# Modulation rows of a two-layer trunk: two short ones in the first stage, the other twenty groups streamed through the first projection

## The chip, the core and the metric

The kernel runs on one core of a Trainium2 chip, in fp32 throughout. The metric is device time in microseconds (us), the median of several executions. The profiler records one execution; a time in its views counts from the start of that execution's span. The engines are TensorE (PE), VectorE (DVE), ScalarE (ACT), GpSimd (POOL) and SyncE (SP), which issues most DMAs here, in program order, and waits in place on semaphores.

## The reference

One step through two layers. For each layer and both condition vectors (one for the 128 prompt tokens, one for the 512 latents) a long vector is made once: six rows of 1024 values.

```
def adaln(cvec, w, b):
    m = jax.nn.silu(cvec) @ w + b
    return jnp.split(m[:, None, :], ADA_CHUNKS, axis=-1)     # w: 1024 x 6144 per layer
...
for l in range(DEPTH):
    mp = adaln(c_ctx[None, :], ada_w[l], ada_b[l])
    ms = adaln(c, ada_w[l], ada_b[l])
    hp = modulate(xp, mp[0], mp[1])                          # x * (1 + scale) + shift
    hs = modulate(xs, ms[0], ms[1])
    ...                                                      # layer 0: mLSTM mixer, layer 1: GLA mixer
    xp = layer_norm(DEEPNORM_ALPHA * xp + mp[2] * yp, ln_mix_g[l], ln_mix_b[l])
    fp = peer_ffn(modulate(xp, mp[3], mp[4]), ...)
    xp = layer_norm(DEEPNORM_ALPHA * xp + mp[5] * fp, ...)
```

Rows 0 and 1 (shift and scale) are wanted at the start of a layer, rows 2 to 5 only after its mixer. `ada_w` is 25.2 MB for each layer.

## The kernel before

The program is a sequence of stages, each with its own semaphores, separated by a barrier of all engines: `mod0` (`modulation_rows`), `proj0`, the mLSTM scan, `out0` (`mixer_output`), `peer0`, then `proj1`, the GLA scan, `out1`, `peer1`. 640 tokens make `NT` = 5 tiles of 128.

`modulation_rows` makes all six rows of layer 0. For each of 12 groups of 512 columns SP loads 128x8x512 of `ada_w` (2 MB) into one of the two slots `m.W[:, s]`, and waits for `ps_full` before it loads a slot again. TensorE multiplies by `cs`, the silu of the two condition vectors (two columns used of 32), in 4 blocks of 128 columns that go to the four 32-column groups of the array: 8 x 4 matmuls of 128x32 by 128x128 a group (L188). VectorE adds the bias (L217). At the end the constants, the tokens `X` (L166 to L168) and the stored rows (L172) close the stage.

`project` (L221) loads the shift and scale rows, broadcast to 128 partitions (L243), modulates each tile on VectorE (L264, L267), transposes it on TensorE (L277, copied by ScalarE, L322), and multiplies it by the weights `w_in`, 6 groups of 512 columns of 2 MB each in the same two slots `m.W` (L249). A unit, below, is one tile by one group: 8 matmuls with 512 columns (L293), 30 units in all, group by group. A slot's next load is issued as soon as `ps_full` says that the group in it is done, one group ahead of its use. Last come the gates (L304). Before unit 0, 1, 2 and 3 TensorE also transposes the next tile. VectorE has nothing to do once the five tiles are modulated.

`mixer_output` normalises each tile on VectorE (`head_norm`), transposes it, multiplies by `w_out` (L825) and adds it to the residual (`residual`: L912 to L915, then the layer norm). In layer 0 it also makes all six rows of layer 1 (`more`): 24 groups of 256 columns of `ada_w`, three slots of 1 MB (L787), 6 groups a tile on TensorE (L839), bias on VectorE (L923); before the stage ends the rows are stored (L797). In layer 1 it does not.

Every fp32 matmul stands in the trace as two records, so a unit is 16 records of L293, and a group of 32 matmuls is 64 records of L188.

Of the kernel before, what the change touches and what calls it, by code (L numbers as in the profile page):

```python
# [18 lines left out]
ALU = mybir.AluOpType  # L19
# [107 lines left out]
def modulation_rows(nc, m, a, layer):  # L127
# [3 lines left out]

    NGRP = CHUNKS * D // HALF
    w = a["ada_w"][layer].rearrange("(k p) n -> p k n", p=P)
    with Stage(nc, f"mod{layer}") as st:
        w_full = [st.sem("w_full0"), st.sem("w_full1")]
        ps_full, row_done, c_loaded, c_step, stored, stream_in, cleared, bias_in = (
            st.sem(n) for n in ("ps_full", "row_done", "c_loaded", "c_step", "stored", "stream_in", "cleared", "bias_in"))
        rows = m.big[:, 0:NGRP * P]
        bias = m.big[:, NGRP * P:2 * NGRP * P]
# [4 lines left out]
        blocks = lambda row: row.rearrange("(g b n) -> b g n", b=4, n=P)  # L144
        at_blocks = lambda x, c: x[c:P:32, :].rearrange("b (g n) -> b g n", n=P)
        block = st.block()

        @block.sync
        def _(sp):
            sp.dma_start(cv, a["c2"]).then_inc(c_loaded, 16)  # L150

            def load(it, first):
                for s in range(2):
                    g = it * 2 + s
                    if not first:
                        sp.wait_ge(ps_full, g - 1)
                    sp.dma_start(m.W[:, s], w[:, :, bass.ds(g * HALF, HALF)]).then_inc(w_full[s], 16)

            load(0, True)
            sp.wait_ge(cleared, 2)  # L160
            for c in range(2):
                sp.dma_start(at_blocks(bias, c), blocks(a["ada_b"][layer])).then_inc(bias_in, 16)
            with sp.Fori(1, NGRP // 2) as it:
                load(it, False)
            if layer == 0:
                sp.dma_start(m.cst[:], a["cst"]).then_inc(stream_in, 16)  # L166
                sp.dma_start(m.X[:, 0, :], a["x_prompt"][0]).then_inc(stream_in, 16)
                sp.dma_start(m.X[:, 1:NT, :], a["x_sample"][0].rearrange("(t p) d -> p t d", p=P))\  # L168
                    .then_inc(stream_in, 16)
            sp.wait_ge(row_done, NGRP)  # L170
            for c in range(2):
                sp.dma_start(blocks(a["rows"][layer, c]), at_blocks(rows, c)).then_inc(stored, 16)  # L172
            sp.wait_ge(stored, 16 * 2)
            sp.wait_ge(stream_in, 48)

        @block.tensor
        def _(pe):
            pe.wait_ge(c_step, 4)

            def products(it, first):  # L180
                for s in range(2):
                    g = it * 2 + s
# [19 lines left out]
        def _(dve):  # L202
# [10 lines left out]
            with dve.Fori(0, NGRP // 2) as it:  # L213
                for s in range(2):
                    g = it * 2 + s
                    dve.wait_ge(ps_full, g + 1)
                    dve.tensor_tensor(rows[:, bass.ds(g * P, P)], m.ps[:, s, 0:P],  # L217
                                      bias[:, bass.ds(g * P, P)], ALU.add).then_inc(row_done, 1)
# [513 lines left out]
def mixer_output(nc, m, a, layer):  # L732
# [12 lines left out]
    more = layer + 1 < LAYERS  # L745
    SLOTS, PER_TILE, WIDTH = 3, 6, 2 * P
    NB4 = WIDTH // 4
    NGRP = CHUNKS * D // WIDTH
    assert NGRP == PER_TILE * (NT - 1)
    ada = a["ada_w"][min(layer + 1, LAYERS - 1)].rearrange("(k p) n -> p k n", p=P)  # L750
    slot = [m.proj[:, s, 0:KD * WIDTH].rearrange("p (k n) -> p k n", k=KD) for s in range(SLOTS)]
    rows, bias = (m.proj[:, SLOTS + n, 0:NGRP * NB4] for n in range(2))
    blocks = lambda row: row.rearrange("(g b n) -> b g n", b=4, n=NB4)
    at_blocks = lambda x, c: x[c:P:32, :].rearrange("b (g n) -> b g n", n=NB4)
    row_ps = lambda q: m.ps[:, 4 + q // 2, (q % 2) * NB4:(q % 2 + 1) * NB4]
    with Stage(nc, f"out{layer}") as st:
# [12 lines left out]
        def _(sp):  # L769
# [11 lines left out]
            if more:  # L781
                def load(n):
# [26 lines left out]
        def _(pe):  # L809
# [34 lines left out]
            if more:  # L844
                tile(1, True)
# [922 lines left out]
```

## Time and profile before

| what | us |
|---|---|
| median of 3 executions (4701.35 to 4704.99) | 4703.77 |
| the profiled execution: device time | 4702.51 |
| its span | 4700.7 |
| first issue in `proj0` | 85.42 |
| first product of `proj0`, L293 | 101.36 |
| gates copied, end of `proj0` | 324.47 |
| first vector instruction of `out0` | 514.31 |
| first vector instruction of `peer0` | 645.65 |

The span is 1.8 us shorter than the device time of the same execution, and that is 1.3 us below the median. The stages that the change touches end at 645.65 us; what is behind it, 4055 us, is the same program before and after. Over the whole span TensorE is busy 80% and VectorE 60%, but these are means over stages with different limits, and each stage has to be read by itself.

### The profile page before, as it was taken

How to read it: one execution, taken by the hardware profiler on the slowest of the kernel's cores; microseconds unless marked ns; L12 is line 12 of the kernel's file. 1: busy time of each engine (PE TensorE's matmuls, PEld its weight loads, DVE VectorE, ACT ScalarE, POOL GpSimd, SP SyncE). 2: the span in 40 equal slices, each digit the busy share in tenths (PEclk: the TensorE clock that was granted, in tenths of full speed). 3: DMA queues.
4: the chain of work that ended last, by engine and by line, in shares of the span. 5: the costliest groups of instructions: out<-in, count | busy, mean ns of one | idle time of the engine just before them, and what ended most of it. 6: DMA issues, size and time to landing. Idle time of an engine off the chain costs nothing. (4 is left out here: it accounts for less than half of the span.)

```text
span 4700.7 us, 50507 instructions
## 1 busy us (share of the span) xinstructions
PE 3752.2 (80%) x13558; PEld 1864.9 (40%) x13558; DVE 2801.3 (60%) x6980; ACT 745.8 (16%) x2098; POOL 2481.2 (53%) x2597
## 2 busy tenths in 40 slices
PE   5987858878888788788879777588878878788877
PEld 3446533333333333343334453333333334333332
DVE  1014566666766676777710366766767676666774
ACT  0111011111111111111110240111111111111211
POOL 0000017767777777777700100576777677777775
PEclk7988889999999999999989779799999999999999
DMA  8101569999999999999941002899999999999998
GB/s 299 54 18 18 184 233 406 405 402 389 407 401 403 389 406 403 398 400 409 407 143 54 19 5 76 308 409 402 404 388 403 401 390 408 400 403 393 409 407 317
DMA packets 456750, 1477.33 MB, mean 314 GB/s; under 512 B 48180, under 2 KB 93940, under 8 KB 456212
## 3 DMA queue, kind: packets, MB, share of 16 engines
q0 software_dynamic: 368640, 1342.34, 72.4%
q1 hardware_dynamic: 87828, 131.85, 8.3%
q8 instruction: 101, 1.65, 0.1%
q14 instruction: 181, 1.48, 0.1%
HBM read 1469.20 MB, written 4.82 MB: 314 GB/s over the span
## 5 line engine op out<-in xcount | busy, mean ns | idle before, releaser
L1651 DVE SCALAR_TENSOR_TENSOR big<-big,ps 128x1024 f32<-128x1024 f32 x1280 | 1559.7, 1219 | 936.0 <-DMA big<-in_peer_u,qk 932.9
L1516 POOL DMA_INDIRECT big<-in_peer_u,qk x1264 | 1198.9, 949 | 393.9 <-issue 294.6
L1414 PE MATMUL ps<-big,y 128*128 128x512 f32 x1280 | 667.1, 676 | 336.2 <-ACT y L1475 256.2
L1523 POOL DMA_INDIRECT big<-in_peer_v,qk x640 | 606.2, 947 | 367.4 <-issue 159.6
L1414 PE MATMUL ps<-mod,diag 128*128 128x512 f32 x1280 | 626.0, 615 | 171.3 <-DMA mod<-in_peer_v,qk 171.3
L1414 PE MATMUL ps<-big,diag 128*128 128x512 f32 x1280 | 617.8, 611 | 161.0 <-DMA big<-in_peer_v,qk 160.2
L1523 POOL DMA_INDIRECT mod<-in_peer_v,qk x640 | 622.4, 973 | 206.6 <-issue 174.3
L1414 PE MATMUL ps<-mod,y 128*128 128x512 f32 x1280 | 567.8, 594 | 10.6 <-DMA mod<-in_peer_v,qk 10.5
L1414 PEld LDWEIGHTS ps<-big,y 128*128 128x128 f32 x1280 | 266.1, 216 | 736.0 <-issue 408.9
L1414 PEld LDWEIGHTS ps<-mod,diag 128*128 128x128 f32 x1280 | 219.6, 189 | 575.7 <-issue 484.1
L1414 PEld LDWEIGHTS ps<-big,diag 128*128 128x128 f32 x1280 | 220.7, 189 | 506.0 <-issue 430.6
L293 PE MATMUL ps<-wrk 128*128 128x512 f32 x960 | 416.3, 595 | 0.0
L1414 PEld LDWEIGHTS ps<-mod,y 128*128 128x128 f32 x1280 | 235.6, 190 | 288.6 <-issue 261.7
L293 PEld LDWEIGHTS ps<-wrk 128*128 128x128 f32 x960 | 183.1, 191 | 227.7 <-issue 227.7
L446 POOL COPY wrk<-big 128x1024 f32 (+1 forms) x5 | 5.2, 1038 | 433.8 <-POOLq L123 325.0
L1023 POOL COPY qk<-big 128x1024 f32 (+1 forms) x10 | 10.3, 1038 | 375.9 <-POOLq L123 261.2
L1475 ACT ACTIVATE y<-cst,qk 128x128 f32<-128x128 f32 x640 | 195.7, 388 | 46.9 <-DVE qk L1668 46.9
L1531 POOL DMA_INDIRECT big<-in_peer_u,qk x16 | 15.7, 982 | 354.0 <-DVE qk L1637 196.0
L1475 ACT ACTIVATE diag<-cst,qk 128x128 f32<-128x128 f32 x640 | 194.4, 386 | 0.0
L825 PE MATMUL ps<-wrk,yT 128*128 128x512 f32 x320 | 146.1, 613 | 13.6 <-ACT yT L859 11.2
L1469 ACT ACTIVATE qk<-qk 128x16 f32<-128x16 f32 x80 | 17.2, 215 | 877.6 <-DVE qk L1661 877.6
L1465 ACT COPY ps<-wrk 128x1024 f32<-128x1024 f32 x38 | 38.6, 1016 | 700.4 <-DVE big L1651 700.4
(320 smaller groups left out, 3458.2 us busy)
## 6 DMA issues: line engine op xcount, KB each, us to landing
wrk<-in_ada_w SPq DMA_DIRECT2D x12, 2048.0 KB, 8.5
big<-in_ada_w SPq DMA_DIRECT2D x24, 1024.0 KB, 5.8
big<-in_peer_u,qk POOLq DMA_INDIRECT x1280, 9.4
mod<-modulation_rows SPq DMA_DIRECT2D x24, 512.0 KB, 10.4
wrk<-in_mlstm_w_in SPq DMA_DIRECT2D x6, 2048.0 KB, 7.9
wrk<-in_gla_w_in SPq DMA_DIRECT2D x6, 2048.0 KB, 7.9
big<-in_peer_v,qk POOLq DMA_INDIRECT x640, 8.7
mod<-in_peer_v,qk POOLq DMA_INDIRECT x640, 9.5
```

The costliest lines, as they stand in the source:

```text
L293: mm = pe.matmul(m.ps[:, u % BANKS, :], m.hT[:, t, k, :], m.W[:, s, k, :], start=k == 0, stop=k == KD - 1)
L446: pool.tensor_copy(qk[d], m.proj[:, t, 0:2 * HALF]).then_inc(pool_[d].sem, 1)
L825: mm = pe.matmul(m.ps[:, 2 + n, :], m.yT[:, k, :], W[:, k, n * HALF:(n + 1) * HALF], start=k == 0, stop=k == KD - 1)
L1023: pool.tensor_copy(qk[d], m.proj[:, t, 0:2 * HALF]).then_inc(pool_[d].sem, 1)
L1414: mm = pe.matmul(m.ps[:, b + h, :], diag[r], ring_v[r % RV][:, h * HALF:(h + 1) * HALF], start=r == 0 and q % 2 == 0, stop=r == TOPK - 1 a ...
L1465: act.copy(xm_ps, xm[t]).then_inc(shown, 1)
L1469: act.activation(tanh[b], t1[b], ACT.Tanh, scale=TANH_SCALE).then_inc(gelu_act.sem, 1)
L1475: act.activation(diag[r], m.ident, ACT.Copy, scale=wv[b][:, r:r + 1]).then_inc(diagonals, 1)
L1516: pool.indirect_dma_start(ring_u[r % RU], None, u, bass.IndirectOffsetOnAxis(ap=expert[q % TURN][:, r:r + 1], axis=0)) \
L1523: pool.indirect_dma_start(ring_v[r % RV], None, v, bass.IndirectOffsetOnAxis(ap=expert[q % TURN][:, r:r + 1], axis=0)) \
L1531: pool.indirect_dma_start(ring_u[r], None, u, bass.IndirectOffsetOnAxis(ap=expert[0][:, r:r + 1], axis=0)) \
L1651: dve.scalar_tensor_tensor(out=ring_u[r % RU], in0=ring_u[r % RU], scalar=1.0, in1=xm_ps, op0=ALU.mult, op1=ALU.mult, accum_out=act_u[q % ...
```

## The change

`modulation_rows` gives way to `first_rows`: only the four groups of shift and scale of layer 0, each with a slot of its own in `m.big`, so that no load waits; the same stage loads the constants, `X` and the first two weight groups of the projection, and waits for all of it. `project_and_rows` takes the place of `project` in layer 0. It does the same 30 units, and besides 20 tasks: task j is one group of 512 columns of the 20 that are left (8 of layer 0, 12 of layer 1). A task's 8 slices of 128 rows of `ada_w` come in two ways. Six go to VectorE (`accumulate`): two halves of three slices, three slots of 0.75 MB, 12 instructions of 128x512 (multiply by the silu value of each partition, one for each condition vector, and add to the accumulators `acc`, two pairs in turn). Two go to TensorE directly (`direct`, 0.25 MB each). `row_sums` then does 16 matmuls with 128 columns: 8 for the two direct slices, 8 with `pick` that sum the accumulators over partitions. `after_unit(j)` says behind which unit the sum of task j stands: 5, 6, 8, 9, 10, 11, 13, 14, 15, 16, 18, 19, 20, 22, 23, 24, 25, 27, 28, 29. `W_BEFORE` says before which task's loads SP issues the weight groups 2 to 5, which units 10, 15, 20 and 25 are the first to use. `mixer_output` makes no rows in either layer. The scan, `project` of layer 1 and both `peer` stages stay.

```diff
+FIRST = 2 * D // HALF
+CHUNK_GROUPS = CHUNKS * D // HALF
...
+def first_rows(nc, m, a):
...
+        slot = [m.big[:, g * KD * HALF:(g + 1) * KD * HALF].rearrange("p (k n) -> p k n", k=KD) for g in range(FIRST)]
...
+            for g in range(FIRST):
+                sp.dma_start(slot[g], w[:, :, g * HALF:(g + 1) * HALF]).then_inc(w_full[g], 16)
...
+                sp.dma_start(at_blocks(bias, c), row_blocks(a["ada_b"][0, 0:2 * D])).then_inc(bias_in, 16)
+            sp.dma_start(m.cst[:], a["cst"]).then_inc(stream_in, 16)
+            sp.dma_start(m.X[:, 0, :], a["x_prompt"][0]).then_inc(stream_in, 16)
+            sp.dma_start(m.X[:, 1:NT, :], a["x_sample"][0].rearrange("(t p) d -> p t d", p=P)).then_inc(stream_in, 16)
+            for s in range(2):
+                sp.dma_start(m.W[:, s], w_in[:, :, s * HALF:(s + 1) * HALF]).then_inc(next_in, 16)
+            sp.wait_ge(row_done, FIRST)
             for c in range(2):
-                sp.dma_start(blocks(a["rows"][layer, c]), at_blocks(rows, c)).then_inc(stored, 16)
...
+            for g in range(FIRST):
+                pe.wait_ge(w_full[g], 16)
+                for k in range(KD):
+                    for b in range(4):
+                        mm = pe.matmul(m.ps[32 * b:32 * b + 32, g, 0:P], cs[:, k, :], slot[g][:, k, b * P:(b + 1) * P],
+                                       start=k == 0, stop=k == KD - 1)
...
+def project_and_rows(nc, m, a):
...
+    tasks = [(0, g) for g in range(FIRST, CHUNK_GROUPS)] + [(1, g) for g in range(CHUNK_GROUPS)]
+    TASKS = len(tasks)
+    KV, KH, SLOTS = 6, 3, 3
+    ada = [a["ada_w"][layer].rearrange("(k p) n -> p k n", p=P) for layer in range(LAYERS)]
+    lnw, mod2 = flat(m.lnw[:]), flat(m.mod[:, 2])
+    slot = [x[:, 0:KH * HALF].rearrange("p (k n) -> p k n", k=KH) for x in (lnw, m.qk, mod2)]
+    quarters = lambda x: [[x[:, (2 * i + n) * HALF:(2 * i + n + 1) * HALF] for n in range(2)] for i in range(2)]
...
+    W_BEFORE = {2: 5, 3: 9, 4: 14, 5: 18}
+    after_unit = lambda j: -(-(320 + 87 * j) // 69)
...
+            for c in range(2):
+                for n in (1, 0):
+                    row = a["rows"][0, c, n * D:(n + 1) * D]
+                    sp.dma_start(m.mod[:, n, c, :], row.partition_broadcast(P)).then_inc(rows_in[c], 16)
+            sp.dma_start(wg, w[:, :, NP_:NP_ + G]).then_inc(wg_full, 16)
+
+            def load_w(g):
+                sp.wait_ge(ps_full, (g - 1) * NT)
+                sp.dma_start(m.W[:, g % 2], w[:, :, g * HALF:(g + 1) * HALF]).then_inc(w_full[g % 2], 16)
+
+            def load_rows_of(j):
+                layer, g = tasks[j]
+                cols = slice(g * HALF, (g + 1) * HALF)
+                for h in range(2):
+                    i = 2 * j + h
+                    if i >= SLOTS:
+                        sp.wait_ge(slot_used, i - SLOTS + 1)
+                    sp.dma_start(slot[i % SLOTS], ada[layer][:, KH * h:KH * (h + 1), cols])\
+                        .then_inc(slot_full[i % SLOTS], 16)
+                if j == 0:
+                    sp.wait_ge(modulated, NT * 2)
+                if j >= 2:
+                    sp.wait_ge(row_full, j - 1)
+                for e in range(2):
+                    sp.dma_start(direct[j % 2][e], ada[layer][:, KV + e, cols]).then_inc(direct_full[j % 2], 16)
+
+            sp.wait_ge(cleared, len(bias_parts))
+            for x, layer, cols in spans(bias_parts):
+                for c in range(2):
+                    sp.dma_start(at_blocks(x, c), row_blocks(a["ada_b"][layer, cols])).then_inc(bias_in, 16)
+            for j in range(TASKS):
+                for g in range(2, NG):
+                    if W_BEFORE[g] == j:
+                        load_w(g)
+                load_rows_of(j)
+            sp.wait_ge(row_done, TASKS)
+            for x, layer, cols in spans(row_parts):
+                for c in range(2):
+                    sp.dma_start(row_blocks(a["rows"][layer, c, cols]), at_blocks(x, c)).then_inc(stored, 16)
+            sp.wait_ge(stored, 16 * 2 * len(row_parts))
...
+            def accumulate(j):
+                if j >= 2:
+                    dve.wait_ge(row_full, j - 1)
+                for k in range(KV):
+                    i = 2 * j + k // KH
+                    if k % KH == 0:
+                        dve.wait_ge(slot_full[i % SLOTS], (i // SLOTS + 1) * 16)
+                    for c in range(2):
+                        part, weight = slot[i % SLOTS][:, k % KH, :], m.silu_c[:, k, c:c + 1]
+                        if k == 0:
+                            ins = dve.tensor_scalar(acc[j % 2][c], part, weight, None, ALU.mult)
+                        else:
+                            dve.wait_ge(acc_done, (j * KV + k - 1) * 2 + c + 1)
+                            ins = dve.scalar_tensor_tensor(out=acc[j % 2][c], in0=part, scalar=weight, in1=acc[j % 2][c],
+                                                           op0=ALU.mult, op1=ALU.add)
+                        ins.then_inc(acc_done, 1)
+                    if k % KH == KH - 1:
+                        dve.wait_ge(acc_done, (j * KV + k + 1) * 2)
+                        dve.sem_inc(slot_used, 1)
+
+            def add_bias(j):
+                dve.wait_ge(row_full, j + 1)
+                if j == 0:
+                    dve.wait_ge(bias_in, 16 * 2 * len(bias_parts))
+                dve.tensor_tensor(at(row_parts, j), m.ps[:, ROW_BANK + j % ROW_BANKS, 0:P], at(bias_parts, j),
+                                  ALU.add).then_inc(row_done, 1)
+
+            for j in range(TASKS):
+                accumulate(j)
+                if j >= 1:
+                    add_bias(j - 1)
+            add_bias(TASKS - 1)
...
+            def row_sums(j):
+                bank = ROW_BANK + j % ROW_BANKS
+                pe.wait_ge(direct_full[j % 2], (j // 2 + 1) * 32)
+                if j >= ROW_BANKS:
+                    pe.wait_ge(row_done, j - ROW_BANKS + 1)
+                else:
+                    pe.wait_ge(copied, NT)
+                for e in range(2):
+                    for b in range(4):
+                        pe.matmul(m.ps[32 * b:32 * b + 32, bank, 0:P], m.silu_c[:, KV + e, :],
+                                  direct[j % 2][e][:, b * P:(b + 1) * P], start=e == 0, stop=False)
+                if j == 0:
+                    pe.wait_ge(picked, 3)
+                pe.wait_ge(acc_done, (j + 1) * KV * 2)
+                for c in range(2):
+                    for b in range(4):
+                        mm = pe.matmul(m.ps[32 * b:32 * b + 32, bank, 0:P], pick[:, c, :],
+                                       acc[j % 2][c][:, b * P:(b + 1) * P], start=False, stop=c == 1)
+                mm.then_inc(row_full, 1)
...
+            def product(u):
+                g, t = u // NT, u % NT
+                if t == 0 and g >= 2:
...
+            transpose(0)
+            done = 0
+            for u in range(NG * NT):
+                product(u)
+                while done < TASKS and after_unit(done) <= u:
+                    row_sums(done)
+                    done += 1
+            pe.wait_ge(wg_full, 16)
+            for t in range(NT):
+                for k in range(KD):
+                    mm = pe.matmul(m.ps[:, 7, t * G:(t + 1) * G], m.hT[:, t, k, :], wg[:, k, :],
+                                   start=k == 0, stop=k == KD - 1)
+            mm.then_inc(ps_full, 1)
+            while done < TASKS:
+                row_sums(done)
+                done += 1
...
 def mixer_output(nc, m, a, layer):
...
-            if more:
-                def load(n):
-                    for s in range(SLOTS):
-                        g = n * SLOTS + s
-                        if not is_first(n):
-                            sp.wait_ge(row_full, g - SLOTS + 1)
-                        sp.dma_start(slot[s], ada[:, :, bass.ds(g * WIDTH, WIDTH)]).then_inc(slot_full[s], 16)
-
...
-                    if rows_too:
-                        row_groups(t, n * PER_TILE // 2)
...
-                if more:
-                    row_groups(t - 1)
...
-                modulation_rows(nc, m, a, layer)
-            project(nc, m, a, layer)
+                first_rows(nc, m, a)
+                project_and_rows(nc, m, a)
+            else:
```

SP's queue at the start of the program, before (the first stage and the start of `proj0`; `wrk` is where the two slots `m.W` lie):

```order
L150 DMA yT<-in_c 128x16
L157 DMA wrk<-in_ada_w 128x8x512 x2
L162 DMA big<-in_ada_b 4x12x128 x2
L163 UNCONDITIONAL_BRANCH
L163 ISA
L157 ISA
L157 DMA wrk<-in_ada_w 128x8x512
```

and now:

```order
L162 DMA yT<-in_c 128x16
L164 DMA big<-in_ada_w 128x8x512 x4
L167 DMA hot<-in_ada_b 4x4x128 x2
L168 DMA cst<-in_cst 128x1572
L169 DMA X<-in_x_prompt 128x1024
L170 DMA X<-in_x_sample 128x4x1024
L172 DMA wrk<-in_mlstm_w_in 128x8x512 x2
L175 DMA modulation_rows<-scr 4x4x128 x2
```

The loop over twelve loads has become four, and the first two weight groups stand in this stage, ahead of the store of the rows.

TensorE's queue in `proj0` around unit 20, now; L407 is a unit's 8 products, L385 and L392 are the two parts of a task's sum. Before, the same stretch held L293 alone. The first row is unit 16:

```order
L407 MATMUL ps<-wrk 128x512 x8
L385 MATMUL ps<-mod,diag 32x128 x8
L392 MATMUL ps<-mod,diag 32x128 x8
L407 MATMUL ps<-wrk 128x512 x16
L385 MATMUL ps<-mod,diag 32x128 x8
L392 MATMUL ps<-mod,diag 32x128 x8
L407 MATMUL ps<-wrk 128x512 x8
L385 MATMUL ps<-mod,diag 32x128 x8
L392 MATMUL ps<-mod,diag 32x128 x8
L407 MATMUL ps<-wrk 128x512 x8
```

These are units 16, 17 and 18, 19 and 20, with the sums of tasks 9, 10 and 11 behind units 16, 18 and 19: the sum of task 11 is the last thing ahead of unit 20.

SP's queue in `proj0` around the load of weight group 4, now; L286 are a task's halves, L293 its two direct slices, L277 is the weight group. Before, weight loads were alone in this queue. The first row belongs to task 12:

```order
L293 DMA mod<-in_ada_w 128x512 x2
L286 DMA mod<-in_ada_w 128x3x512
L286 DMA lnw<-in_ada_w 128x3x512
L293 DMA mod<-in_ada_w 128x512 x2
L277 DMA wrk<-in_mlstm_w_in 128x8x512
L286 DMA qk<-in_ada_w 128x3x512
L286 DMA mod<-in_ada_w 128x3x512
```

The weight group of unit 20 stands behind the direct slices of task 13, whose wait is `row_full` >= 12, and so behind the sum of task 11.

## Rows read from the trace of the kernel before

**Rows 1.** The page: the costliest group, in the two `peer` stages.

```profile
L1651 DVE SCALAR_TENSOR_TENSOR big<-big,ps 128x1024 f32<-128x1024 f32 x1280 | 1559.7, 1219 | 936.0 <-DMA big<-in_peer_u,qk 932.9
```

**Rows 2.** Timeline of SP: start, us taken, what, how many.

```profile
69.42 0.49 SPq L168 DMA_DIRECT2D X<-in_x_sample  x1
79.58 1.14 SPq L172 DMA_DIRECT2D modulation_rows<-big  x2
85.42 1.76 SPq L243 DMA_DIRECT2D mod<-modulation_rows  x4
```

**Rows 3.** DMA of the first 85 us: GB/s in 40 slices, median us to landing.

```profile
GB/s 4 204 406 392 386 387 255 337 403 364 400 390 96 356 406 375 389 379 53 302 405 388 386 386 202 390 400 380 391 333 341 406 308 384 400 419 397 411 412 96
X<-in_x_sample SPq DMA_DIRECT2D x1, 2048.0 KB, 14.8
```

**Rows 4.** Timeline of the start of `proj0`, on VectorE and TensorE.

```profile
96.98 1.23 DVE L267 TENSOR_TENSOR y<-y,mod 128x1024 f32<-128x1024 f32 x1
99.59 1.97 PE L277 MATMUL ps<-cst,y 128*128 128x128 f32 x8 [3.99 <-DMA wrk<-in_mlstm_w_in]
101.36 8.23 PE L293 MATMUL ps<-wrk 128*128 128x512 f32 x16
119.50 1.23 DVE L267 TENSOR_TENSOR y<-y,mod 128x1024 f32<-128x1024 f32 x1
```

**Rows 5.** Timeline of SP and of TensorE, weight load behind unit 4 and last instructions.

```profile
139.87 34.71 SPq L249 DMA_DIRECT2D wrk<-in_mlstm_w_in  x2
311.19 13.25 PE L304 MATMUL ps<-yT,wrk 128*128 128x16 f32 x80
```

**Rows 6.** Timeline of VectorE in `out0`: first and last L912, first of `peer0`.

```profile
542.55 1.22 DVE L912 TENSOR_TENSOR big<-ps,mod 128x1024 f32<-128x1024 f32 x1 [14.00 <-PE ps L825]
633.10 1.22 DVE L912 TENSOR_TENSOR big<-ps,mod 128x1024 f32<-128x1024 f32 x1 [12.84 <-PE ps L825]
645.65 1.22 DVE L1561 SCALAR_TENSOR_TENSOR wrk<-mod,X 128x1024 f32<-128x1024 f32 x1 [3.81 <-PEq L123]
```

**Rows 7.** The same in `out1` and `peer1`.

```profile
2869.25 1.22 DVE L912 TENSOR_TENSOR big<-ps,mod 128x1024 f32<-128x1024 f32 x1 [13.60 <-PE ps L825]
2933.08 1.23 DVE L912 TENSOR_TENSOR big<-ps,mod 128x1024 f32<-128x1024 f32 x1 [7.61 <-PE ps L825]
2942.10 1.23 DVE L1561 SCALAR_TENSOR_TENSOR wrk<-mod,X 128x1024 f32<-128x1024 f32 x1 [0.87 <-PEq L123]
```

**Rows 8.** Windows: length, busy us of PE, PEld, DVE, ACT, POOL, clock, DMA, GB/s.

```profile
40.40:42.50 2.10, 1.96 (x64) 1.69 (x64) 0.00 (x0) 0.00 (x0) 0.00 (x0) 1.00 0.88 305
35.10:38.90 3.80, 3.64 (x64) 3.00 (x64) 0.00 (x0) 0.00 (x0) 0.00 (x0) 0.50 0.88 330
```

**Rows 9.** Groups by form on VectorE: busy us, mean ns of one.

```profile
L645 DVE SCALAR_TENSOR_TENSOR mod<-big,scr 128x512 f32<-128x512 f32 x5 | 3.4, 684 | 0.0
L679 DVE SCALAR_TENSOR_TENSOR mod<-mod,scr,ps 128x256 f32<-128x256 f32 x4 | 1.6, 475 | 0.0
L720 DVE TENSOR_SCALAR big<-big,stat 128x1024 f32<-128x1024 f32 x5 | 4.1, 812 | 0.2
L897 DVE TENSOR_SCALAR y<-wrk,scr 128x256 f32 x12 | 4.1, 409 | 0.1
```

**Rows 10.** DMA issues, 85 to 325 us: count, KB each, median us to landing.

```profile
wrk<-in_mlstm_w_in SPq DMA_DIRECT2D x6, 2048.0 KB, 7.9
```

**Rows 11.** Timeline of TensorE in `out0`: first matmuls behind an idle stretch, and later.

```profile
521.28 1.97 PE L816 MATMUL ps<-cst,y 128*128 128x128 f32 x8 [9.29 <-DVE y L906]
524.44 10.08 PE L825 MATMUL ps<-wrk,yT 128*128 128x512 f32 x16 [1.19 <-ACT yT L859]
535.30 7.13 PE L825 MATMUL ps<-wrk,yT 128*128 128x512 f32 x16 [0.78 <-DMA wrk<-in_mlstm_w_out]
```

**Rows 12.** Timeline of VectorE beside a GpSimd copy, in the mLSTM scan.

```profile
341.77 1.05 POOL L446 COPY mod<-big 128x1024 f32 x1
341.88 1.49 DVE L621 TENSOR_TENSOR wrk<-wrk,scr 128x512 f32<-128x512 f32 x1
```

More of the change, by code:

```diff
@@ L150, in _ @@
             sp.dma_start(cv, a["c2"]).then_inc(c_loaded, 16)
[L152 to L159, printed above, removed]
+            for g in range(FIRST):
+                sp.dma_start(slot[g], w[:, :, g * HALF:(g + 1) * HALF]).then_inc(w_full[g], 16)
             sp.wait_ge(cleared, 2)
             for c in range(2):
[L162 to L170, printed above, removed]
+                sp.dma_start(at_blocks(bias, c), row_blocks(a["ada_b"][0, 0:2 * D])).then_inc(bias_in, 16)
[5 more added lines that the diff above has]
+            sp.wait_ge(row_done, FIRST)
             for c in range(2):
-                sp.dma_start(blocks(a["rows"][layer, c]), at_blocks(rows, c)).then_inc(stored, 16)
+                sp.dma_start(row_blocks(a["rows"][0, c, 0:2 * D]), at_blocks(rows, c)).then_inc(stored, 16)
             sp.wait_ge(stored, 16 * 2)
             sp.wait_ge(stream_in, 48)
+            sp.wait_ge(next_in, 32)
         @block.tensor
@@ L212, in _ @@
             dve.wait_ge(bias_in, 16 * 2)
-            with dve.Fori(0, NGRP // 2) as it:
-                for s in range(2):
[L215 to L218, printed above, removed]
+            for g in range(FIRST):
+                dve.wait_ge(ps_full, g + 1)
+                dve.tensor_tensor(rows[:, g * P:(g + 1) * P], m.ps[:, g, 0:P], bias[:, g * P:(g + 1) * P],
+                                  ALU.add).then_inc(row_done, 1)
@@ L744, in mixer_output @@
     var = m.scr[:, 8:12]
[L745 to L755, printed above, removed]
     with Stage(nc, f"out{layer}") as st:
@@ L809, in _, with tile @@
         def _(pe):
-            def tile(t, rows_too):
+            def tile(t):
                 first = is_first(t)
@@ L917, in residual @@
                 layer_norm(nc, dve, m, rest, rest_act, t, z, m.X[:, t, :], "added", passed)
-            def row_groups(t):
-                for q in range(0, PER_TILE, 2):
-                    g = (t - 1) * PER_TILE + q
-                    dve.wait_ge(row_full, g + 2)
-                    dve.tensor_tensor(rows[:, bass.ds(g * NB4, 2 * NB4)], m.ps[:, 4 + q // 2, 0:2 * NB4],
-                                      bias[:, bass.ds(g * NB4, 2 * NB4)], ALU.add).then_inc(row_done, 1)
             head_norm(0)
```

173 lines of the change are left out of this document (112 added, 61 removed).

## The prediction

> **What bounds the kernel now.** I read the chain of work that ended last first: it lies almost wholly in the two `peer` stages, whose costliest group waits for gathered rows [rows 1]. The change leaves them alone, so the question is what the first 646 us become. For those I read timelines, stage by stage, asking at the end of each which wait ended last.
>
> The first stage is bound by transfers. SP issues loads as slots come free, the last, `X`, at 69.42; it lands 14.8 us later, at 84.2, and `proj0` issues its first load at 85.42 [rows 2, 3]. TensorE and VectorE have short bursts between loads. In `proj0` the bound turns: after the first product at 101.36 TensorE runs without a gap to the gates at 311.19, that is 209.8 us for 30 units [rows 4, 5]. VectorE finishes the fifth tile at 120.7 and then idles, and weight loads come a whole group ahead (group 2 is issued at 139.87, behind unit 4, for use in unit 10) [rows 4, 5]. `out0` is bound by neither alone: tile after tile, TensorE does a tile and six row groups, and VectorE waits for it. From the first L912 to the last it takes 90.55 us, and to the first instruction of `peer0` another 12.55 [rows 6]. `out1` is the same stage without row groups: 63.83 and 9.02 [rows 7].
>
> The fifth unit ends near 139.6, as the load issued behind it shows, so a unit is (311.19 - 139.6) / 25 = 6.86 us [rows 5].
>
> **The change part by part.**
>
> *The first stage.* It now moves 8.4 MB of `ada_w`, 0.8 of constants, 2.6 of `X` and 4.2 of projection weights: 16.0 MB, issued without a wait between. In the stage before, the slices without a dip read 375 to 419 GB/s, and dips to 53 to 255 stand where the slots were refilled [rows 3]. I take 395: 40.5 us, and 2.7 us before bytes flow (slices are 2.1 us, the second is half full), so the last lands at 43.2. The store of the rows stands behind the weights in the queue; with the 1.2 us from landing to the next stage's issue and one more for the store, `proj0` starts at 45.5, not 85.42: -39.9. Bounds: the mean of all 40 slices with their dips, 338, gives 47.3 us and -33; 406 throughout gives -41.
>
> The Trainium skill states a limit that speaks against this term (DMA: Bandwidth & Descriptors, "Where 436 GB/s comes from"): for transfers from HBM to SBUF the HBM side binds at about 358 GB/s for each core. By it 16.0 MB take an estimated 44.7 us, and the whole change comes out 4 us slower than I forecast. The slices above 400 in [rows 3] don't bear it out on this one core.
>
> *The start of `proj0`.* The weights are there, so the transposes of tile 1 no longer wait for them. They began at 99.59, though the tile was ready at 96.98 + 1.23 = 98.21 [rows 4]: -1.4. The eight bias loads and the gate weights stand ahead of the task loads in SP's queue, but VectorE is busy with tiles until 19.4 us past the first product; nothing waits for them. If they were late, the slack of task 0 (its sum stands behind unit 5, at about 45 us) would still cover it.
>
> *The rows taken from `out0`.* I give it `out1`'s cadence: 90.55 - 63.83 = 26.7, and at its end, where rows were stored, 12.55 - 9.02 = 3.5 [rows 6, 7]: -30.2, give or take 1. VectorE's work for a tile is the same in both layers.
>
> *The sums on TensorE.* A sum is 16 matmuls, 32 records of 128 columns. 64 such records took 1.96 us at clock 1.00 and 3.64 at 0.50 [rows 8], so a sum costs 0.98 to 1.82. Units before it are dense, so I take 0.98: 20 sums, +19.6. The upper end would be +36.
>
> *The products on VectorE.* A task is 2 openers and 10 multiply-adds of 128x512. Lower bound: half of L720's 812 ns, and L645's 684: 2 x 0.41 + 10 x 0.68 = 7.7. Upper: L897 gives 409 ns at 256 columns, which with L720 makes 0.54 at 512, and L679, with a scalar for each partition and a PSUM operand, 475 at 256, so some 0.75 at 512: 8.5, and a bias add under 0.41 [rows 9]. 7.7 to 8.9. I charge nothing, and this is what hides it: task j may begin when sum j-2 is done, and sum j stands at least two units and a sum later, 14.7 us. That leaves 6 us for late halves. Without cover each us more on a task would cost up to 20.
>
> *The weight groups in the shared queue.* This is the term that costs most. SP issues group g only once it has passed the direct slices of the task before, and these wait for `row_full`. By the order rows group 4 stands behind task 13's slices, which wait for the sum of task 11, and that sum stands between units 19 and 20. Unit 20 is the first to use group 4. So TensorE finishes the sum, SP only then issues two slices of 0.25 MB and the 2 MB, and TensorE stands meanwhile. Group 5 is the same: task 17's slices wait for the sum of task 15, right behind unit 24. Groups 2 and 3 are issued after the sums of tasks 2 and 6, behind units 8 and 13, one unit and one sum (7.8 us) ahead of use. A load takes 7.9 us to land [rows 10]; the 0.5 MB ahead of it adds 1.3 at 395 GB/s: 9.2 from the end of the sum. Waits: 9.2 twice, and 9.2 - 7.8 = 1.4 twice: +21.2. Bounds: 7.9 to 11 (if the half behind it, 0.75 MB, shares its bandwidth), so 16 to 28. Before, the same loads had four units of slack more.
>
> *What the clock adds.* After 9.29 us idle TensorE's transposes took 1.97 us, and the next 16 records 10.08, where later ones took 7.13 [rows 11]: 2.95 more, at 1.2 GHz for part of it. The two long waits are as long: +5.9. The short waits should cost nothing, as the 7.13 after 0.78 idle shows.
>
> *The end of `proj0`.* The last sum stands behind unit 29, ahead of the gates' 13.25 us [rows 5]; the bias add and eight small stores run beside them. Two such stores, with the barrier, took 5.8 us in the first stage [rows 2]; six more issues at 0.57 make 9.3. Free; without the gates they would cost those 9.3.
>
> *Sum.* -39.9 - 1.4 - 30.2 + 19.6 + 21.2 + 5.9 = -24.8. The profiled execution took 4702.5, which gives 4677.7; it lies 1.3 below the median: 4679.
>
> **Rivals.**
>
> *A: the weights come in time.* If I misread what holds SP, the waits and the clock's share go: 4679 - 27 = 4652. For it: before, weights were never late after unit 0. Against it: the order rows leave no path by which group 4 could be issued ahead of that sum. 0.12.
>
> *B: every sum waits.* A sum needs VectorE, DMA and the bias add of the sum before last. If each costs a handover like the 1.19 us that L825 waits for ScalarE [rows 11], that is 20 x 1.19 = +24: 4703, no change. Against it: 6 us of slack a task. 0.12.
>
> *C: the four column blocks of a sum don't overlap.* 8 records of 128x128 took 1.97 at 1.2 GHz [rows 11], so 0.12 each at full clock: 32 make 3.9, or +59 over 20 sums: 4738. Against it: [rows 8], 0.03 a record. 0.03.
>
> *D, on the other side: VectorE becomes the bound.* Beside a GpSimd copy one instruction of 128x512 took 1.49 us, over twice its 0.68 [rows 12]. With ten of these a task takes 16 us, and since the tasks start 19.4 us past the first product, the last ends at 19.4 + 20 x 16 = 339, where I expect the last sum at 209.8 + 19.6 + 27.1 = 257: +82, or 4761. It decides from 11.9 us a task, and makes the kernel slower from about 13. For it: a new load on VectorE beside 400 GB/s into SBUF. Against it: GpSimd has only four memsets here, before the tiles; and L1651, beside gathers all the time, takes 1219 ns for 1024 columns [rows 1], no more than L267's 1.23 in [rows 4]. 0.07.
>
> **How the numbers follow.** Forecast 0.66, A 0.12, B 0.12, C 0.03, D 0.07. The forecast's own bounds: start -41 to -33, `out0` -31 to -29, sums 19.6 to 26, waits 16 to 28, clock 3 to 7: taken together at their ends 4668 and 4702, and more likely 4668 to 4692. The range reaches down to A at 4652 and up to most of B, 4701; C, D and part of B stay out. A measurement of this kernel can tell about 0.2%, 9.4 us, from no change: faster below 4694.4 (forecast, A and a little of B) 0.80, between 0.10, slower (C and D) 0.10.
>
> **What would show it.** First load of `proj0` at 44 to 49; first product 14.5 after it. TensorE idle for DMA `wrk<-in_mlstm_w_in` about 9 us before units 20 and 25, with the clock at 0.5 after each, and 1 to 2 before units 10 and 15. The two lines of the sums together 20 us busy. VectorE's idle time in `proj0` waiting for TensorE, not the reverse. L912 in `out0` 16 us apart. Wrong would be: no idle TensorE before unit 20 (A), a wait before most sums (B, D), or sums near 4 us (C).

## The result, and the profile after

The changed kernel takes 4690.18 us (median of 9, 4687.59 to 4694.09) where the kernel before takes 4703.77 (median of 9, 4701.35 to 4708.76): ratio 0.997, 95% interval 0.996 to 0.998. That is 13.6 us less, about half of the 24.8 forecast, and inside the range. The profiled execution took 4688.81 us with a span of 4687.0.

SP's timeline after: start, us taken, what, how many. It answers to [rows 2].

```profile
19.02 13.09 SPq L172 DMA_DIRECT2D wrk<-in_mlstm_w_in  x2
32.16 4.32 SPq L175 DMA_DIRECT2D modulation_rows<-scr  x2
47.22 1.77 SPq L272 DMA_DIRECT2D mod<-modulation_rows  x4
```

`proj0` begins at 47.22 instead of 85.42. SP is held 13 us on the two weight loads, which took it 2.75 us in the kernel before (from 87.22); 11.8 MB are already issued here, and that this is what holds SP is my reading, not tested. The store of the rows goes out behind them. What SP waits for last in this stage (us in total, times, longest; L178 is its wait for the weights), and the landing of the two weight loads:

```profile
SPq L178 <- DMA wrk<-in_mlstm_w_in: 9.8, 1, 9.8
DMA to landing us min/median/max: 21.9/23.2/24.6
```

SP's last issue, a store, ends at 36.48, and 9.8 us later is 46.3; the second weight load, issued at 21.7, lands 24.6 us later, at 46.3 too. So the trace puts the end of the stage on the weights and not on the store. The DMA view of the first 47 us, GB/s in 40 slices, answers to [rows 3]:

```profile
GB/s 0 17 132 370 401 404 392 389 390 382 387 385 387 389 389 396 370 385 389 385 397 390 411 391 420 408 401 404 392 389 383 389 383 389 383 390 389 197 42 0
```

No dips are left: 370 to 420 GB/s from the fourth slice to the last but three. The Trainium skill's limit of about 358 GB/s for transfers from HBM (DMA: Bandwidth & Descriptors, "Where 436 GB/s comes from") is not what binds this one core: the 34 slices from the fourth on read 391 on average.

TensorE in `proj0`, its timeline around the four weight groups and at both ends:

```profile
61.88 8.61 PE L407 MATMUL ps<-wrk 128*128 128x512 f32 x16
...
143.05 8.83 PE L407 MATMUL ps<-wrk 128*128 128x512 f32 x16 [3.49 <-DMA wrk<-in_mlstm_w_in]
...
187.21 8.83 PE L407 MATMUL ps<-wrk 128*128 128x512 f32 x16 [3.23 <-DMA wrk<-in_mlstm_w_in]
...
220.00 7.13 PE L407 MATMUL ps<-wrk 128*128 128x512 f32 x16
227.06 0.65 PE L385 MATMUL ps<-mod,diag 128*32 128x128 f32 x16
227.52 0.62 PE L392 MATMUL ps<-mod,diag 128*32 128x128 f32 x16
240.15 10.00 PE L407 MATMUL ps<-wrk 128*128 128x512 f32 x16 [12.01 <-DMA wrk<-in_mlstm_w_in]
...
293.39 8.99 PE L407 MATMUL ps<-wrk 128*128 128x512 f32 x16 [11.14 <-DMA wrk<-in_mlstm_w_in]
...
334.41 13.90 PE L421 MATMUL ps<-yT,wrk 128*128 128x16 f32 x80
```

The first product is at 61.88 (101.36 before), the gates at 334.41 (311.19 before). Units 10, 15, 20 and 25 wait for their weights, 3.5, 3.2, 12.0 and 11.1 us, and each of these units then takes 8.83 to 10.00 us instead of 7.13. SP at the third of these places:

```profile
228.20 0.82 SPq L293 DMA_DIRECT2D mod<-in_ada_w  x2
229.06 0.43 SPq L277 DMA_DIRECT2D wrk<-in_mlstm_w_in  x1
229.54 0.58 SPq L286 DMA_DIRECT2D qk<-in_ada_w  x1
```

This is the chain that the prediction names: the sum ends at 228.1, the direct slices go out at 228.20, the weights at 229.06, and unit 20 starts at 240.15. The line that issues these weights (L277) gives their landing:

```profile
DMA to landing us min/median/max: 10.2/10.5/11.0
```

Windows around unit 10 (the first two) and through the wait before unit 20: length, busy us of PE, PEld, DVE, ACT and POOL, granted clock, DMA share, GB/s.

```profile
142.00:144.00 2.00, 0.95 (x2) 0.64 (x3) 0.00 (x0) 0.00 (x0) 0.00 (x0) 0.89 1.04 383
144.00:146.00 2.00, 2.00 (x3) 0.68 (x2) 0.87 (x3) 0.00 (x0) 0.00 (x0) 0.50 1.05 393
...
228.00:230.00 2.00, 0.14 (x8) 0.00 (x0) 1.85 (x6) 1.07 (x1) 0.00 (x0) 1.00 0.47 114
230.00:232.00 2.00, 0.00 (x0) 0.00 (x0) 2.00 (x4) 0.00 (x0) 0.00 (x0) 1.00 0.86 303
232.00:234.00 2.00, 0.00 (x0) 0.00 (x0) 1.79 (x4) 0.00 (x0) 0.00 (x0) 0.58 0.98 302
234.00:236.00 2.00, 0.00 (x0) 0.00 (x0) 2.00 (x4) 0.00 (x0) 0.00 (x0) 0.50 0.94 340
236.00:238.00 2.00, 0.00 (x0) 0.00 (x0) 0.30 (x1) 0.00 (x0) 0.00 (x0) 0.50 1.05 403
238.00:240.00 2.00, 0.00 (x0) 0.00 (x0) 0.00 (x0) 0.00 (x0) 0.00 (x0) 0.50 1.06 394
...
244.00:246.00 2.00, 2.00 (x3) 0.72 (x3) 0.00 (x0) 0.00 (x0) 0.00 (x0) 0.51 0.00 0
246.00:248.00 2.00, 2.00 (x6) 0.92 (x5) 0.00 (x0) 0.00 (x0) 0.00 (x0) 1.00 0.00 0
```

While TensorE stands, the granted clock falls from 1.00 to 0.50 (2.4 to 1.2 GHz), and it is back only some 6 us after the unit has begun. Behind the short wait before unit 10 it falls to 0.50 as well. Between 228 and 240 the queues move 3.7 MB (the GB/s column, 2 us each), while the two direct slices and the weight group are 2.6 MB: the rest belongs to the row halves that SP issued behind the weights.

VectorE in `proj0`, by group: busy us, mean ns of one, idle before. They answer to the prices in [rows 9].

```profile
L345 DVE SCALAR_TENSOR_TENSOR mod<-lnw,diag,mod 128x512 f32<-128x512 f32 x70 | 47.6, 746 | 1.5 <-DVE mod L345 1.5
L342 DVE TENSOR_SCALAR mod<-lnw,diag 128x512 f32<-128x512 f32 x14 | 6.1, 480 | 5.0 <-DMA lnw<-in_ada_w 5.0
```

`out0`, the first and last L1092 (L912 before) and the first instruction of `peer0`, answer to [rows 6]:

```profile
569.11 1.22 DVE L1092 TENSOR_TENSOR big<-ps,mod 128x1024 f32<-128x1024 f32 x1 [14.34 <-PE ps L1020]
632.93 1.23 DVE L1092 TENSOR_TENSOR big<-ps,mod 128x1024 f32<-128x1024 f32 x1 [7.60 <-PE ps L1020]
641.89 1.23 DVE L1728 SCALAR_TENSOR_TENSOR wrk<-mod,X 128x1024 f32<-128x1024 f32 x1 [0.81 <-PEq L123]
```

63.82 and 8.96 us, `out1`'s numbers [rows 7]. From 540.53, its first vector instruction, `out0` takes 101.4 us instead of 131.3.

Up to `peer0` the two traces differ by only 645.65 - 641.89 = 3.8 us, though their spans differ by 13.7. The rest stands in stages that are the same program (`peer0` -1.8, the GLA scan -2.2, `peer1` -5.6). Whether the change did this was the first thing to try.

### The profile page after: what moved, and what is told of

The parts are those of the page before. It is cut to its first block and busy times, and to the rows that moved or that the text cites. A ratio compares the mean times of both kernels' runs of the same rounds, so it can differ in the third digit from the quotient of the medians.

```text
span 4687.0 us, 47842 instructions
## 1 busy us (share of the span) xinstructions
PE 3731.2 (80%) x12150; PEld 1839.4 (39%) x12150; DVE 2952.0 (63%) x7223; ACT 746.4 (16%) x2098; POOL 2499.9 (53%) x2600
## 5 line engine op out<-in xcount | busy, mean ns | idle before, releaser
L1690 POOL DMA_INDIRECT mod<-in_peer_v,qk x640 | 632.6, 988 | 205.1 <-issue 177.0
L407 PE MATMUL ps<-wrk 128*128 128x512 f32 x480 | 221.4, 618 | 29.9 <-DMA wrk<-in_mlstm_w_in 29.9
L1190 POOL COPY qk<-big 128x1024 f32 (+1 forms) x10 | 10.4, 1041 | 373.7 <-POOLq L123 261.0
L525 PE MATMUL ps<-wrk 128*128 128x512 f32 x480 | 207.3, 594 | 0.0
L1642 ACT ACTIVATE diag<-cst,qk 128x128 f32<-128x128 f32 x640 | 194.5, 386 | 0.0
```

The source lines that it names most:

```text
L407: mm = pe.matmul(m.ps[:, u % BANKS, :], m.hT[:, t, k, :], m.W[:, g % 2, k, :], start=k == 0, stop=k == KD - 1)
L525: mm = pe.matmul(m.ps[:, u % BANKS, :], m.hT[:, t, k, :], m.W[:, s, k, :], start=k == 0, stop=k == KD - 1)
L1642: act.activation(diag[r], m.ident, ACT.Copy, scale=wv[b][:, r:r + 1]).then_inc(diagonals, 1)
L1690: pool.indirect_dma_start(ring_v[r % RV], None, v, bass.IndirectOffsetOnAxis(ap=expert[q % TURN][:, r:r + 1], axis=0)) \
```

## The experiments

Each is compared with the kernel before on the same chip; "over early_weights" compares medians. Lengths of `proj0` in traces run from its first issue to the scan's first issue. The runs were made on three chips, on which the kernel before has medians of 4703.56 us (before_again to all_on_tensor), 4709.32 (first_only to later_loads) and 4704.71 (the last two). So a difference of medians across these groups can be some us off, and the lengths in traces are the firmer measure.

**before_again**: the kernel before once more, for its trace.

> The kernel before once more, for its trace. The stages up to the first instruction of peer0 end 3.8 us earlier in the changed kernel's trace (641.89 against 645.65), but the whole span is 13.7 us shorter. Theory 1: the other 10 us, in stages that the change leaves alone (peer0 -1.8, scan of layer 1 -2.2, peer1 -5.6), are scatter between executions; then this trace's peer stages and scans differ from those of the first trace of before by several us. Theory 2: the change shortens the later stages; then this trace repeats 1751.4 and 1758.7 us for the two peer stages and 188.9 for the mLSTM scan to within 1 us.

4709.13 us, one execution, span 4707.3. `peer0` 1748.5 us, `peer1` 1756.2, mLSTM scan 191.4, where the first trace has 1749.6, 1758.6 and 188.9 in the same measure. Over all the traces of this study, whatever the kernel, `peer0` takes 1746.2 to 1752.2, `peer1` 1753.1 to 1759.5, the GLA scan 199.1 to 201.5, the mLSTM scan 188.5 to 194.5. Theory 2 fails, since this trace doesn't repeat the first to within 1 us, and the stages scatter. The changed kernel's 1753.1 for `peer1` and 199.1 for the GLA scan stand at the low end, with other traces within 0.1 us of each. With two traces of the kernel before, a shift of a us or two by the change is not excluded. `out0` scatters too, in the kernel before: 138.7 instead of 131.3. TensorE's timeline of `out0` in this trace shows most of why:

```profile
569.10 1.10 PE L839 MATMUL ps<-big,diag 128*32 128x64 f32 x64 [1.85 <-DMA big<-in_ada_w]
570.13 1.73 PE L816 MATMUL ps<-cst,y 128*128 128x128 f32 x8
572.96 9.25 PE L825 MATMUL ps<-wrk,yT 128*128 128x512 f32 x16 [1.10 <-ACT yT L859]
...
597.75 1.94 PE L816 MATMUL ps<-cst,y 128*128 128x128 f32 x8 [0.19 <-issue]
600.79 8.99 PE L825 MATMUL ps<-wrk,yT 128*128 128x512 f32 x16 [1.10 <-ACT yT L859]
```

Two units took 9.25 and 8.99 us instead of 7.13, and the transposes before them (L816) 1.73 and 1.94 instead of 1.09 and 1.06, behind short waits for the rows of layer 1: 5.5 of the 7.4 us. The rest is in the waits. In the nine traces whose `out0` has no rows in it, it takes 101.3 to 102.2. So the trace of before on which the prediction rests held a short `out0`; against this second one the changed kernel is 13.6 us ahead at `peer0` (655.47 against 641.89).

**early_weights**: SP issues the weight groups earlier, and that is all.

```diff
-    W_BEFORE = {2: 5, 3: 9, 4: 14, 5: 18}
+    W_BEFORE = {2: 3, 3: 7, 4: 11, 5: 15}
```

> The weight groups 2 to 5 are issued before tasks 3, 7, 11 and 15 instead of 5, 9, 14 and 18, nothing else. Theory 1 (the waits of TensorE for weights, 29.9 us, and the slower units behind them, 8.1 us, come only from where the loads stand in SP's queue): both go, 38 us, 4652. No wait for wrk<-in_mlstm_w_in, units all 7.1. Rival (the transfers of the rows are what is short: moving one load forward only makes another late): TensorE waits before sums for mod<-in_ada_w or VectorE instead, and the gain is under 15 us, 4675 or more.

4656.26 us, ratio 0.990 (0.988 to 0.992), 33.9 below the changed kernel. `proj0` took 262.9 us instead of 302.2: 39.2 gone. From first product to gates it is 234.5 instead of 272.5, 38.0. TensorE's timeline at unit 20:

```profile
216.16 0.64 PE L385 MATMUL ps<-mod,diag 128*32 128x128 f32 x16
216.63 0.62 PE L392 MATMUL ps<-mod,diag 128*32 128x128 f32 x16
217.18 7.13 PE L407 MATMUL ps<-wrk 128*128 128x512 f32 x16
```

No wait, no slow unit, and nothing takes their place: the loads still need 10.4 us to land, now beside a whole group's work. The expectation of 38 holds in `proj0`, the rival's falls. The whole gained less than 38, and the traces show where: `peer0`, the GLA scan and `peer1` took 9.4 us more together than in the trace of the changed kernel, and their spans differ by 31.6.

**double_sums**: as early_weights, with each sum's matmuls made twice. The waits for VectorE now stand ahead of the whole sum.

```diff
-                for e in range(2):
+                for again in range(2):
+                    for e in range(2):
...
```

> As early_weights, with the 16 matmuls of each of the 20 sums done twice (the result is the same). Theory 1: a sum costs TensorE 1.0 us of matmuls and 0.2 of change-over; the second pass costs 20 x 1.0 = 20 us over early_weights, 4672. Rival (sums are partly hidden in gaps that TensorE has anyway): under 8 us. Rival (each pass pays its own change-over and drains): 24 us or more.

4673.97 us, ratio 0.994 (0.992 to 0.996), 17.7 over early_weights, 0.88 a sum. The trace at unit 6's sum:

```profile
115.19 0.65 PE L389 MATMUL ps<-mod,diag 128*32 128x128 f32 x16
115.66 0.62 PE L393 MATMUL ps<-mod,diag 128*32 128x128 f32 x16
116.09 0.62 PE L389 MATMUL ps<-mod,diag 128*32 128x128 f32 x16
116.53 0.62 PE L393 MATMUL ps<-mod,diag 128*32 128x128 f32 x16
117.08 7.13 PE L408 MATMUL ps<-wrk 128*128 128x512 f32 x16
```

The second pass moves the next unit by 0.87 us (from its last records to the next start it is 0.55 in both kernels). So the sums lie wholly on the path: 0.88 for the matmuls. The rest of a sum's cost is change-over: in early_weights a unit with a sum behind it takes 8.07 us (217.18 to 225.25) where a unit alone takes 6.87, so 1.2 in all, 0.3 of it at the change.

**all_on_tensor**: as early_weights, with all eight slices multiplied on TensorE, none on VectorE.

```diff
+                for k in range(KV):
+                    for b in range(4):
+                        mm = pe.matmul(m.ps[32 * b:32 * b + 32, bank, 0:P], m.silu_c[:, k, :],
+                                       slot[i % SLOTS][:, k % KH, b * P:(b + 1) * P], start=k == 0, stop=False)
...
-                accumulate(j)
```

> As early_weights, but VectorE makes no products: TensorE multiplies all 8 slices of a task, 32 matmuls (as the kernel before did) instead of 16. Theory 1: 20 x 0.98 = 20 us more than early_weights, 4672, if the slots are refilled in time. Rival (taking the products to VectorE buys nothing, since a sum's cost is mostly fixed): within 5 us of early_weights. Second rival (slots that stay occupied until the sum make loads late): more than 30 us, with waits for lnw, qk or mod <-in_ada_w.

4673.68 us, ratio 0.994 (0.992 to 0.995), 17.4 over early_weights, with one wait of 1.2 us for a slice. A unit with its sum takes 8.95 us in that trace instead of 8.07: 0.88 for 16 more matmuls, 17.6 for 20 tasks. `proj0` is 20.1 longer, the wait and 1.4 us in the gates included. So the products on VectorE are worth some 17 us, what 16 matmuls a task cost, and no more.

**first_only**: one part alone. The first stage and 8 tasks, `out0` with the rows of layer 1 as before.

```diff
-    tasks = [(0, g) for g in range(FIRST, CHUNK_GROUPS)] + [(1, g) for g in range(CHUNK_GROUPS)]
+    tasks = [(0, g) for g in range(FIRST, CHUNK_GROUPS)]
-    W_BEFORE = {2: 5, 3: 9, 4: 14, 5: 18}
-    after_unit = lambda j: -(-(320 + 87 * j) // 69)
+    W_BEFORE = {2: 2, 3: 4, 4: 5, 5: 7}
+    after_unit = lambda j: 6 + 3 * j
```

> One part alone: the first stage and the streaming of the 8 groups of layer 0 (one sum behind every third unit, weights in time), while the rows of layer 1 stay in out0 as before. Theory 1: the start is 39.5 us earlier, 8 sums cost 8 x 1.2 = 10, so proj0 ends 30 us earlier; out0 keeps its 131 to 139 us: 4674. Rival (the parts are not additive: out0 with the rows in it loses or wins with what lies ahead of it): out0 outside 131 to 139 in the trace.

4672.10 us, ratio 0.992 (0.990 to 0.994). Its `proj0` took 248.0 us, 14.95 less than early_weights for 12 sums less (1.25 each), and its `out0` 134.2, inside the 131 to 139 of before. The parts add up: moving layer 1's rows as well costs 15 us in `proj0` and saves 30 to 37 in `out0` (101.4 against the 131.3 and 138.7 of before).

**vector_plus4, vector_plus8**: as early_weights, with 4 or 8 more VectorE instructions in each task from the third on; their result goes to a tile that is not used.

```diff
+                        for extra in range(2 if j >= 2 else 0):     # 4 in vector_plus8
+                            dve.scalar_tensor_tensor(out=m.y[:, o:o + HALF], in0=m.X[:, 1, 0:HALF], scalar=weight,
+                                                     in1=m.X[:, 0, 0:HALF], op0=ALU.mult, op1=ALU.add)
```

> As early_weights, with 4 more VectorE instructions of 128x512 (their result is not used) in each task from the third on: a task takes 8.0 + 4 x 0.68 = 10.7 us of VectorE instead of 8.0. The prediction's claim (6 us of slack a task): no change from early_weights, 4656. Rival (the slack is that of the chain, not of a task: from the first sum at 46 us past the first product on, 18 tasks follow one another, 46 + 18 x 10.7 = 239 against 234 for TensorE's own work): 5 us more, 4661, and TensorE waits for VectorE before some of the sums.

> The same with 8 more, 13.4 us a task. If VectorE's chain is the bound: last sum at 46 + 18 x 13.4 = 287 us past the first product instead of 234, so 53 us more than early_weights, 4709, slower than the kernel before. If a task's own slack of 6 us were what counts, 5.4 more would still be hidden: 4656.

4 more: 4657.19 us, ratio 0.989 (0.987 to 0.990), `proj0` 263.2 us, no wait of TensorE. 8 more: 4702.88 us in one execution, `proj0` 311.3, 48.3 longer. Waits of TensorE for VectorE in that trace: in total, times, longest.

```profile
PE ps L403 <- DVE mod L348: 29.4, 10, 4.6
```

Of the 48.3 us 29.4 are waits for VectorE. Behind them TensorE's clock is down again, at 0.50 in the window 196 to 201 around the line below; the slower matmuls there make most of another 14.7, and the gates 4.2 (17.25 us instead of 13.05).

```profile
197.02 1.08 PE L403 MATMUL ps<-mod,diag 128*32 128x128 f32 x16 [4.46 <-DVE mod L348]
```

VectorE's bias adds show what a task took, back to back (vector_plus4 first, vector_plus8 behind it):

```profile
274.60 0.27 DVE L367 TENSOR_TENSOR scr<-ps,diag 128x128 f32<-128x128 f32 x1
284.87 0.27 DVE L367 TENSOR_TENSOR scr<-ps,diag 128x128 f32<-128x128 f32 x1
...
302.88 0.27 DVE L367 TENSOR_TENSOR scr<-ps,diag 128x128 f32<-128x128 f32 x1
315.80 0.27 DVE L367 TENSOR_TENSOR scr<-ps,diag 128x128 f32<-128x128 f32 x1
```

10.27 and 12.92 us, where 10.7 and 13.4 were expected. From the first sum to the last, TensorE leaves (294.9 - 107.8) / 18 = 10.4 us for each of 18 tasks. So vector_plus4 is hidden, but only just, and it doesn't tell the two theories apart: with the measured 10.27 the chain of tasks forecasts no loss either. vector_plus8 does: 18 x (12.92 - 10.4) = 45 us, and from first product to gates it took 44.1 more. The chain of tasks counts, and not the slack of one.

**later_loads**: as early_weights, with weight group 1 and the tokens of tiles 2 to 4 loaded in `proj0`.

```diff
-            sp.dma_start(m.X[:, 1:NT, :], a["x_sample"][0].rearrange("(t p) d -> p t d", p=P)).then_inc(stream_in, 16)
+            sp.dma_start(m.X[:, 1, :], a["x_sample"][0, 0:P, :]).then_inc(stream_in, 16)
...
+            sp.dma_start(m.X[:, 2:NT, :], a["x_sample"][0, P:, :].rearrange("(t p) d -> p t d", p=P)).then_inc(x_in, 16)
+            sp.dma_start(m.W[:, 1], w[:, :, HALF:2 * HALF]).then_inc(w_full[1], 16)
```

> As early_weights, but the first stage loads only what the start of proj0 needs: weight group 1 (2.1 MB) and the tokens of tiles 2 to 4 (1.6 MB) are loaded in proj0, ahead of the row tasks. Theory 1 (the first stage is bound by bytes): 3.7 MB at 380 GB/s, 9.7 us less, 4646. Rival (they are then late in proj0: VectorE waits for X, or the tasks' first halves come late): under 4 us gained.

4647.01 us, ratio 0.987 (0.985 to 0.989), 9.3 less than early_weights. SP's timeline:

```profile
37.55 1.75 SPq L272 DMA_DIRECT2D mod<-modulation_rows  x4
```

`proj0` starts at 37.55 instead of 46.68 and is as long as in early_weights, 263.0. The first stage is bound by bytes: 9.1 us for 3.7 MB is 400 GB/s.

**seven_slices**: as early_weights, with seven slices of a task on VectorE and one on TensorE.

```diff
-    KV, KH, SLOTS = 6, 3, 3
+    KV, KH, SLOTS = 7, 4, 3
```

> As early_weights, but VectorE takes 7 of a task's 8 slices (14 instructions, about 9.4 us) and TensorE 1, so a sum has 12 matmuls instead of 16. Theory 1: VectorE has the room (10.7 us a task cost nothing), and a sum is 8 records of 31 ns shorter: 20 x 0.25 = 5 us less than early_weights, 4651. Rival (the slots of 1 MB instead of 0.75, in the order 4 and 3 slices, come late or VectorE holds the sums up): no gain or a loss, with waits of TensorE before sums.

4646.82 us, ratio 0.988 (0.986 to 0.989); `proj0` took 257.5 us, 5.5 less, with no wait before a sum. The first part of a sum in its timeline:

```profile
113.44 0.42 PE L386 MATMUL ps<-mod,diag 128*32 128x128 f32 x8
```

The median is 9.4 below early_weights; 5.5 of it is in `proj0`, and I take the rest for the scatter of the later stages (its four times lie from 4640.78 to 4647.58).

**later_and_seven**: both.

> later_loads and seven_slices together. If both gains are independent (bytes of the first stage, matmuls of proj0): 4647 - 5 = 4642. Rival (the later loads push the first tasks back by some us, which VectorE with 9.4 us a task can't make up): 4647 or more.

4637.57 us, ratio 0.986 (0.984 to 0.988): `proj0` starts at 37.6 and takes 257.5 us. Both gains are there in full. It is 67 us below the kernel before on its chip (4704.71), and nothing of the computation is left out.

## Why the prediction came out as it did

- **The start**: -39.9 and -1.4 forecast, 41.3; measured 101.36 - 61.88 = 39.5. The mechanism holds, and the rate nearly (391 against 395 GB/s). [rows 3] also has slices of 302 to 364, which I counted neither as full nor as dips; with no slot to wait for, none came here. The 1.7 us by which `proj0` starts late are in the landing: the weights land at 46.3, not 43.2, though the DMA view shows few bytes moving after 44. I gave the store behind them a us more, and the trace doesn't put the end of the stage on the store. Why the last bytes trail is open. later_loads shows the stage bound by bytes.
- **`out0`**: -30.2 forecast, -30.0 between the two traces. Right by size for that trace. What I could not see in one trace is that the kernel before can pay 7 us more, as it does in before_again.
- **The sums**: 19.6 forecast, 24.3 measured (1.2 each; early_weights and double_sums). The matmuls cost even less than I took, 0.88; the term was mis-sized because [rows 8] show bursts that begin from rest, and not the change from a dense unit to a sum and back, 0.3 us each.
- **The products on VectorE**: 7.7 to 8.9 us a task forecast, 8.2 measured from one bias add to the next in a row, hidden. The argument for it was wrong in one point: I gave each task 6 us of slack, and vector_plus8, whose tasks take 4.8 us more (12.92), lost 48. What counts is the pace of TensorE from the first sum to the last, 10.4 us a task in early_weights; in the changed kernel with its waits it is (333.9 - 108.5) / 18 = 12.5. Rival D's 11.9, worked out as if the tasks could run from the start without the sums, is not far from that. Rival D had its mechanism right and its condition absent.
- **The weight groups**: this step named the chain exactly, and was mis-sized. 21.2 forecast, 29.9 measured, above my own bound of 28. From the end of the sum the weights took 12.0 us before unit 20, where I had 9.2: 0.9 until SP has issued the two slices ahead of them, and then 10.2 to 11.0 to land. The 7.9 of [rows 10] is a load with no other beside it; here the halves of the next task share its bandwidth (3.7 MB moved where 2.6 were ahead or its own). I had put this in the bound only, and SP's time for the two slices nowhere. It counts four times.
- **The clock**: 5.9 forecast for the two long waits; measured 2.87 and 1.86 behind these, and 1.7 behind each short one, where I had 0: 8.1. Those waits came out at 3.2 to 3.5 us rather than 1.4, and the windows show the clock at 0.50 behind them. That a wait of 1.4 would have cost nothing is not shown either: in before_again it fell behind waits of 1.8.
- **The sum**: in `proj0`, from first product to gates, 46.7 forecast and 272.5 - 209.8 = 62.7 measured: 29.9 + 8.1 + 24.3, and 0.4 from a slower first unit. These 16.0 us and 2.0 at start and `out0` are why the trace gains 6.8 and not 24.8 by these terms; 3.0 more are in the end of `proj0` (0.8) and in a longer mLSTM scan (2.2, scatter): 3.8. That the medians differ by 13.6 is scatter in the stages that are the same, and the short `out0` of the first trace. That the measured time is as near the forecast as it is, is in part luck: by the terms alone the gain is 6.8 us, a quarter of the forecast, and with it the kernel would stand near 4697. How much of the 13.6 is owed to each is open: two traces of before can't say what `out0` takes on average.
- **Rival A** was the world of early_weights: it put 4652, and 4656.26 was measured there. **B** and **C** are excluded by the trace: no sum waits, and 32 records take about 1 us.

## What to carry to other kernels

When a load joins a queue whose entries wait on another engine's progress, work out at which instruction of that engine the load can be issued, and compare it with the instruction that needs it: here a table of four numbers cost 34 us of a gain of 47. A load's time to land must be taken from a place as busy as the one where it will stand. One trace of the kernel before is not its average: here a single stage differed by 7 us between two. Work moved onto an idle engine is worth only what the busy engine is spared (17 us), and the saving is lost from the point where the idle engine's chain becomes the longer one. That point comes from the whole chain of tasks, not from the slack of one.

## What the hardware showed that I had not expected

- Waits of 3.2 to 3.5 us were followed by units of 8.83 us at a clock partly at 1.2 GHz, against 7.13; a wait of 1.85 us in before_again stood ahead of a unit of 9.25 us. Behind 0.78 us there was nothing of it [rows 11], and in the first trace of before waits of 1.77 and 1.82 us at the same places left the clock at 1.00 and the units at 7.13. So the length of a wait alone doesn't decide.
- A VectorE multiply-add of 128x512 with a scalar for each partition takes 746 ns, and one with a constant and other operands 684 [rows 9]; in a row they start 0.66 us apart (four more made a task 2.65 us longer between vector_plus4 and vector_plus8).
- Between a dense unit of 128x512 matmuls and a group with 32 columns of weights TensorE loses about 0.3 us, there and back, without any wait in the trace.
- TensorE's clock fell to 0.50 while it was at work without a pause: in the gates, 80 records of 128x16, of early_weights. The gates took 12.1 to 17.3 us over the traces; how much of that is the clock was not tested.

```profile
297.00:300.00 3.00, 3.00 (x30) 3.00 (x29) 0.00 (x0) 0.00 (x0) 0.00 (x0) 1.00 0.09 23
303.00:306.00 3.00, 3.00 (x16) 3.00 (x16) 0.00 (x0) 0.00 (x0) 0.00 (x0) 0.50 0.00 0
```
